# HGRN2 layer of a streaming encoder step: low parts of the heads' outputs made head by head, kept in DRAM and loaded back for the output projection

## The reference

```python
q, f, i, g = split(rms_norm(x) @ w_in[1], 4)          # (544, 2048) @ (2048, 8192)
o = rms_norm(hgrn2(silu(q), (1 - lb) * sigmoid(-f), i, logf, S0)) * silu(g)
x = x + o @ w_out[1]                                  # (544, 2048) @ (2048, 2048)
```

## Time and profile before

| | |
|---|---|
| median of three runs | 2265.87 us (2264.69 to 2266.54) |
| profiled execution, its own time | 2268.73 us |
| its span, first to last instruction | 2267.0 us |
| PE busy | 98% of the span |
| DVE, ACT, POOL busy | 71%, 50%, 3% |
| mean granted clock of PE | 0.994 |
| moved by DMA | 225 MB, a mean of 99 GB/s |

### The profile page before, as it was taken

One profiled execution on the slowest core, in us unless ns is written; L12 is line 12 of the kernel. 1 busy time (PEld: TensorE's weight loads), 2 busy tenths in 40 slices (PEclk: granted clock), 3 DMA queues, 4 the chain that ended last, 5 costly groups with the idle time before them and its releaser, 6 DMA issues.

```text
span 2267.0 us, 43518 instructions
## 1 busy us (share of the span) xinstructions
PE 2213.8 (98%) x17257; PEld 2187.6 (96%) x17257; DVE 1609.6 (71%) x2647; ACT 1138.5 (50%) x1552; POOL 71.5 (3%) x75
## 2 busy tenths in 40 slices
PE   7999999999999999999999999999999999998999
PEld 6999999999999998999999999999999999998999
DVE  7888888888888887522477777777777777776221
ACT  6766566656656666522444444444444444443221
POOL 5000000000000000301000000000000000000000
PEclk9999999999999999999999999999999999999999
DMA  7433333333333336354422222222222222213442
GB/s 257 139 95 95 95 97 108 103 111 95 97 99 98 109 97 192 91 151 115 131 84 70 77 77 77 75 71 78 77 74 72 77 77 77 70 39 100 120 118 81
DMA packets 394470, 224.98 MB, mean 99 GB/s; under 512 B 9523, under 2 KB 378726, under 8 KB 394342
## 3 DMA queue, kind: packets, MB, share of 16 engines
q1 hardware_dynamic: 344342, 189.83, 29.6%
q10 hardware_dynamic: 50032, 33.81, 4.7%
HBM read 195.04 MB, written 28.56 MB: 99 GB/s over the span
## 4 chain that ended last, share of the span: by engine, by line
PE 83%; DVE 7%; ACT 5%; issue 3%; DMA 0%; ACTq 0%; DVEq 0%
PE psum L666 49%; PE psum L873 20%; ACT work L1018 3%; PE psum L789 3%; PE psum L656 2%; DVE work L1583 1%; PE psum L764 1%; PE psum L712 1%; DVE w_lo L1454 1%; PE psum L738 1%; DVE w_chain L1474 1%; PE psum L748 1%; ACT w_hi L1018 1%; PE psum L835 1%; PE psum L814 1%
## 5 line engine op out<-in xcount | busy, mean ns | idle before, releaser
L666 PE MATMUL psum<-act_hi,w_hi 128*128 128x272 f32 x3200 | 678.7, 293 | 9.9 <-DVE act_lo L1540 5.3
L666 PE MATMUL psum<-act_lo,w_hi 128*128 128x272 f32 x3200 | 662.5, 288 | 0.0
L666 PE MATMUL psum<-act_hi,w_lo 128*128 128x272 f32 x3184 | 661.0, 289 | 0.0
L1018 ACT ACTIVATE w_hi<-w_raw 128x1024 fp32r<-128x1024 f32 x350 | 366.2, 1055 | 452.3 <-PE psum L666 256.7
L666 PEld LDWEIGHTS psum<-act_hi,w_hi 128*128 128x128 f32 x3200 | 504.7, 190 | 12.5 <-DVE act_lo L1540 4.3
L666 PEld LDWEIGHTS psum<-act_lo,w_hi 128*128 128x128 f32 x3200 | 505.0, 189 | 0.0
L666 PEld LDWEIGHTS psum<-act_hi,w_lo 128*128 128x128 f32 x3184 | 499.9, 190 | 0.0
L1448 DVE TENSOR_TENSOR w_lo<-w_raw,w_hi 128x1024 fp32r<-128x1024 f32 x199 | 249.1, 1252 | 304.7 <-ACT w_hi L1018 304.5
L1018 ACT ACTIVATE work<-work 128x544 f32<-128x544 f32 (+6 forms) x336 | 235.1, 732 | 285.9 <-DVE work L1698 189.2
L873 PE MATMUL psum<-act_hi,w_hi 128*128 128x272 f32 x960 | 278.7, 290 | 1.8 <-DVE w_lo L1454 1.0
L873 PE MATMUL psum<-act_hi,w_lo 128*128 128x272 f32 x960 | 276.9, 288 | 0.0
(11 more groups left out here) (271 smaller groups left out, 3133.8 us busy)
## 6 DMA issues: line engine op xcount, KB each, us to landing
w_raw<-in_w_in SPq DMA_DIRECT2D x241, 512.0 KB, 4.1
w_raw<-in_w_out SPq DMA_DIRECT2D x64, 512.0 KB, 6.4
out<-work ACTq DMA_DIRECT2D x48, 256.0 KB, 4.4
x_residual<-work ACTq DMA_DIRECT2D x32, 272.0 KB, 3.7
work<-x_residual SPq DMA_DIRECT2D x32, 272.0 KB, 3.0
w_chain<-in_w_in SPq DMA_DIRECT2D x15, 512.0 KB, 4.5
full<-x_residual SPq DMA_DIRECT2D x8, 544.0 KB, 7.2
o_spill<-work ACTq DMA_DIRECT2D x15, 272.0 KB, 2.1
```

The source lines that it names most:

```text
L666: mm = pe.matmul(acc[par][:, j, :], at, a[:, k, j * HT:(j + 1) * HT], start=(k == 0 and n == 0), stop=(k == KT - 1 and n == 2))
L1018: return nc.scalar.activation(out, in_, f, **kw)
```

## The change

ACT and DVE now make the low part of head h's output in the loop, when the head is done: `put_o_lo` on ACT makes the high part into a tile of its own (`o_part_hi`), `o_lo_part` on DVE subtracts it from the output into `o_part_lo`, and ACT issues a store of that to a new DRAM tensor `o_lo_spill`. SP loads the low parts of heads 0 to 14 back into `act_lo`, in four loads of up to 4 heads each, between the third and the fourth half of w_out, once the input projections are done and the store of the heads in question has landed. PE waits for these loads (`o_back`) and for `act_hi` in place of `act_lo_ready`. DVE's 15 low parts beside the last head are gone; ACT still makes the 15 high parts there, and k tile 15 is made as before. The DMA scratch area is set to 8192 bytes.

```diff
--- before.py
+++ after.py
@@ -96,9 +96,6 @@
              {-1: [], 0: [], 1: range(0, 4), 2: [4, 5], 3: [6, 7, 8], 4: [9, 10], 5: [11, 12], 6: [13, 14]}]
 
 
-LAST_REST = {0: range(0, 4), 1: range(4, 8), 2: [8, 9], 3: [10, 11], 4: [12], 5: [13, 14]}
-
-
 class Chain:
 
 
@@ -128,6 +125,7 @@
                  hgrn_norm_w, hgrn_lb, y_prompt, y_sample, k_prompt, v_prompt, s_prompt, k_sample, v_sample,
                  s_sample):
     x_residual = nc.dram_tensor("x_residual", (KT, P, T), F32, kind="Internal").ap()
+    o_lo_spill = nc.dram_tensor("o_lo_spill", (H, P, T), F32, kind="Internal").ap()
     o_spill = nc.dram_tensor("o_spill", (H, P, T), F32, kind="Internal").ap()
 
     with ExitStack() as ctx:
@@ -154,6 +152,8 @@
 
         Y = sb("Y", [P, 4, T])
         rstd_x = sb("rstd_x", [P, T])
+        o_part_hi = sb("o_part_hi", [P, T], F32R)
+        o_part_lo = sb("o_part_lo", [P, T], F32R)
 
         ident = sb("ident", [P, P])
         ident_b = sb("ident_b", [P, P], BF16)
@@ -328,6 +328,7 @@
 
         o_ready = sem("o_ready"); o_stored = sem("o_stored"); o_back = [sem(f"o_back{i}") for i in range(4)]
         run_on_ready = sem("run_on_ready")
+        o_part_hi_ready = sem("o_part_hi_ready"); o_part_lo_ready = sem("o_part_lo_ready")
 
         x_back = [sem(f"x_back{i}") for i in range(4)]; row_scaled = sem("row_scaled")
         diff_made = sem("diff_made"); diff_hi_ready = sem("diff_hi_ready"); diff_lo_ready = sem("diff_lo_ready")
@@ -546,6 +547,14 @@
                                 load_o(u)
                         else:
                             half(i * 4 + (out0 + u), u, src)
+                        if l == 1 and first and u == 2:
+                            sp_eng.wait_ge(half_done, OUT_BASE[1])
+                            for m in range(4):
+                                heads = slice(4 * m, min(4 * m + 4, H - 1))
+                                sp_eng.wait_ge(o_stored, 16 * (H - 1 + heads.stop))
+                                sp_eng.dma_start(act_lo[:, heads, :].bitcast(F32),
+                                                 o_lo_spill[heads].rearrange("k p t -> p k t")
+                                                 ).then_inc(o_back[m], 16)
                     if l == 0 and first:
                         load_o(2)
                         load_o(3)
@@ -658,7 +667,13 @@
             def part(slot, par, ks, wait_act=None, first_lo=False):
 
                 for k in ks:
-                    if wait_act is not None:
+                    if wait_act == 3 * KT:
+                        pe.wait_ge(act_hi_ready, wait_act + k + 1)
+                        if k < KT - 1:
+                            pe.wait_ge(o_back[k // 4], 32)
+                        else:
+                            pe.wait_ge(act_lo_ready, wait_act + 1)
+                    elif wait_act is not None:
                         pe.wait_ge(act_lo_ready, wait_act + k + 1)
                     for n, (w, a) in enumerate(((w_hi, act_hi), (w_hi, act_lo), (w_lo, act_hi))):
                         for j in range(2):
@@ -1246,6 +1261,15 @@
                 act.wait_ge(r_cum, h + 1)
                 func(eb, cum, ACT.Exp).then_inc(r_eb, 1)
 
+            def put_o_lo(h):
+
+                act.wait_ge(o_ready, h + (H + 1))
+                func(o_part_hi[:], full[:, bass.ds(h, 1), :].rearrange("p a t -> p (a t)"), ACT.Copy
+                     ).then_inc(o_part_hi_ready, 1)
+                act.wait_ge(o_part_lo_ready, h + 1)
+                act.dma_start(o_lo_spill[bass.ds(h, 1)].rearrange("a p t -> (a p) t"), o_part_lo[:].bitcast(F32)
+                              ).then_inc(o_stored, 16)
+
             def rec_norm(h):
 
                 act.wait_ge(r_ssq, h + 1)
@@ -1357,6 +1381,7 @@
                             rec_next(h + 1, u)
                             if u == 7:
                                 rec_decays(h + 1)
+                                put_o_lo(h)
                         ch.leave(H - 1)
 
                 g0 = OUT_BASE[l]
@@ -1768,6 +1793,13 @@
                 group(h, 0, 1)
                 dve.wait_ge(r_kde, h + 1)
                 dve.tensor_tensor(kd, kd, kk, ALU.mult).then_inc(r_kd, 1)
+
+            def o_lo_part(h):
+
+                dve.wait_ge(o_part_hi_ready, h + 1)
+                dve.wait_ge(o_stored, h * 16 + 16 * (H - 1))
+                dve.tensor_tensor(o_part_lo[:], full[:, bass.ds(h, 1), :].rearrange("p a t -> p (a t)"),
+                                  o_part_hi[:].bitcast(F32), ALU.subtract).then_inc(o_part_lo_ready, 1)
 
             def rec_dve(h, u):
                 if u == 0:
@@ -1976,6 +2008,7 @@
                             if u == 7:
                                 rec_gate(h)
                                 rec_distances(h + 1)
+                                o_lo_part(h)
                         ch.leave(H - 1)
                     evacuate(l, H - 1, 3)
                 g0 = OUT_BASE[l]
@@ -1991,8 +2024,6 @@
                         rec_dve(H - 1, u)
                     if l == 0 and u == -1:
                         act_split(KT, range(DVE_SPLITS))
-                    elif l == 1 and u in LAST_REST:
-                        act_split(3 * KT, LAST_REST[u])
                     if u == 1:
                         lo(g0 + 3, 3)
                     if u == 4 - l:
@@ -2001,7 +2032,8 @@
                         lo(g0 + 5, 1)
                 if l == 1:
                     rec_gate(H - 1)
-                dve.wait_ge(act_lo_ready, (2 * l + 2) * KT - 1)
+                if l == 0:
+                    dve.wait_ge(act_lo_ready, (2 * l + 2) * KT - 1)
                 act_split((2 * l + 1) * KT, [KT - 1])
 
                 def out_pair(l, i, first=False, last=False):
@@ -2041,7 +2073,7 @@
     import concourse.bacc as _bacc
     from concourse.bass_utils import run_bass_kernel_spmd as _run
 
-    nc = _bacc.Bacc("TRN2", target_bir_lowering=False, num_devices=1)
+    nc = _bacc.Bacc("TRN2", target_bir_lowering=False, num_devices=1, dynamic_dma_scratch_size=8192)
     arrays, args = {}, []
     for name in _INS:
         a = _np.ascontiguousarray(inputs[name])
```

## The result

The changed kernel takes 2272.3 us in the median of 9 runs (2269.46 to 2274.43), the kernel before 2266.69 us in 9 runs beside it. The ratio is 1.0024 with a 95% interval of 1.0015 to 1.0034: 5.4 us slower, between 3.4 and 7.7 us. The forecast was 2269.5 us, 3.6 us slower, which was counted as "no change that can be told". The measured time lies inside the stated range (2264.0 to 2273.5 us), but above the forecast's own (2267.5 to 2270.4 us). The profiled execution took 2272.3 us with a span of 2270.6 us.

The account below looks back on a forecast made before the run. PE's waits in the tail after the loop were taken as the bound. The late fourth half costs 4.4 us, less 0 to 1.6 us of low clock: 2265.87 + 3.6 = 2269.5 us, range 2264.0 to 2273.5 us.

Parts of the forecast that it names:

- What bounds the kernel: PE's waits in the tail, the 53 us after the loop: 11.7 us, nowhere else; DVE's low parts some 5.2 us of the chain.
- What it adds in the loop: Per looped head: ACT's Copy, wait and store issue, DVE's subtraction; ACT 2.4 us late, absorbed by idle time, cost nothing.
- What it adds in the tail, on ACT: Ahead of ACT's first tail work: Copy, wait for DVE's subtraction and store issue move everything on ACT by 2.4 us.
- What it moves on SP: Fourth w_out half queues behind the reloads and head 14's store in the tail, landing at about 2048.7.
- L: Time the fourth w_out half lands in the tail: forecast 2048.7, upper bound 2050.4, lower bound 2046.4.
- The sum: Tail, up to the third level scores: 4.4 us later, less 0 to 1.6 us of low clock; middle 3.6 us.
- behind that nothing changes: After the third level scores: no further change, as last low parts lie in DVE's waits and later chains start at PE.
- Of the 5.2 us taken away nothing is left: Tail: 2.4 us of the relief goes to ACT's delay, the rest was never alone on the path.
- Faster: Rival, tail: DVE's low parts are the bound; 5.2 us plus 1.5 us of low clock return, 2259.2 us; chance 0.10.
- Slower: Rival, ACT's high part in the tail: fourth half lands still later, cost 4.6 to 6.2 us, 2271.3 us; chance 0.31.
- In between: Rival, tail: store shares engines with the loads, half lands at 2046.4, cost 0.6 to 2.2 us, 2267.3 us; chance 0.15.
- Slower in the loop: Rival, loop: ACT's wait for DVE reaches PE in each head, 1 us each, 2281 us; chance 0.04.

Follow-up runs that it names:

- e10: The kernel before with the tail's 15 low parts left out and nothing in their place (result wrong): ratio 0.9985 to the kernel before.
- e2: e1 with the wait for the low part and the store's issue moved from ACT to SP: ratio 0.9984 to the kernel before.
- e1: The changed kernel with SP issuing the fourth w_out half ahead of the four reloads of low parts: ratio 1.0007 to the kernel before.
- e3: The kernel before plus only the loop's new steps; low parts stored, never loaded, and made again in the tail: ratio 1.0012 to the kernel before.
- e9: e2 with the fifth half's split later, its low part behind the third-level placing, and ACT's high parts 4 to 7 behind the kd copies: ratio 0.9961.
- e5: The changed kernel with head 14's low part made by DVE in the tail, so SP's last reload needs no wait for its store: ratio 1.0003.

## Why the prediction was right or wrong

With these runs the tail's 4.70 us can be taken apart by differences: the relief alone is -4.88 (e10); the loop's steps and the reloads, with the store on SP and the half early, +1.49 (e2 less e10); ACT's wait for DVE and its issue of the store +3.48 (e1 less e2); the half behind the reloads +4.61 (the change less e1). The sum is +4.70 by construction. By the ratios the same parts are -3.4, -0.2, +5.2 and +3.9 us, each with some 3 us of doubt. So the signs of the relief, of ACT's delay and of the late half stand, their sizes within 1 or 2 us; the +1.49 isn't shown.

**What bounds the kernel: right.** Waits appeared and went in the tail alone. In the whole loop of the HGRN2 layer PE shows no wait in the kernel before, after, in e1, e2, e3 or e9.

**What it adds in the loop, costed at nothing: right.** The cover was what the step named: ACT's 3.59 us ahead of the third half's high part fell to 1.04 (2.55 us, where 2.4 were taken), DVE's 3.15 to 0.60. There is 0.6 to 1 us of cover left. Moving the store to SP brought no wait of PE in the loop either. The smaller DMA scratch, taken at nothing too, wasn't tried alone.

**What it adds in the tail, on ACT, 2.4 us: right.** The copies of v start 6.43 us after the turns, before 3.80: 2.6 us.

**What it moves on SP: right, to half a microsecond.** L was put at 2048.7, 17.8 us after the turns of v; the half landed 18.2 us after them (2041.96 + 6.06). The store of head 14 took 5.91 us, where 5.8 were taken and 2.1 was the other end. The doubt between "one behind the other" and "shared engines" was put at 2.3 us (2048.7 less 2046.4; worked out again, 4.98 MB at 370 GB/s from 2032.4 on end at 2045.9, so it was 2.8), and in e5, which takes SP's wait for the store away (and 0.27 MB of reloads), the half came 2.3 us sooner. ACT's wait is 4.17 us (some 4 forecast), PE's new wait 5.91 (some 5), the sums over the own scores come 5.0 us later (4.4). e1 confirms the step by undoing it: 4.61 of 4.70 us.

**The sum, "the third level scores run 4.4 us later, less 0 to 1.6 us": this is the step that failed.** They run 5.98 us later against the turns of v. The term that I subtracted was the low clock, "which now would fall earlier, on L814". It fell earlier, as forecast, but it didn't end there: the granted clock is 0.50 from 2048 to 2058, all the way through L829, L833 and the k tiles behind, where the earlier trace rows has it for the 2 us after the wait only. From L833 to the third level scores it takes 15.08 us, before 14.13. The term had the wrong sign, +1.0 us instead of -0.8. The other 0.6 us are the landing (0.4) and the way from there to the own sums (0.2). What the clock costs shows in the k tiles between: at 0.50, 20 matmuls run in 4.00 us (2054 to 2058); at 0.95, 15 run in 2.00 us. Behind the third level scores 1.28 us come back, as the clock is low for a shorter time there than in the profiled execution of before. The step "behind that nothing changes" didn't have that either, and e3, e5 and e10 show the same 1.3 to 1.5 us there, so it more likely belongs to that one execution of before than to the change. That makes the 4.70 us of the tail, against 3.6 forecast: a miss of 2.4 us at the third level scores, and it is luck that half of it was made up behind them.

**"Of the 5.2 us taken away nothing is left … the rest was never alone on the path": right for the waits, without the clock.** In e10 only 1.9 of the 5.2 us come back as a wait, ahead of the own sums. The wait ahead of the third level scores is 2.66 us with and without the low parts, since there the fifth half's high part waits for PE, as the prediction says. What it left out is the low clock behind the wait that shrinks, 1.5 us more up to the third level scores. The rival "Faster" had the low parts as the bound, with 5.2 us and 1.5 us of clock; e10 shows its clock and 1.9 of its 5.2 us. e2 nearly meets its two conditions, with the half there in time and ACT 0.5 us late instead of 2.6, and gains 3.4 us in the tail and 3.6 by the ratio, about half of the 6.7 that the rival named. My sum didn't depend on this, since it followed the chain of the change itself, from the store to the third level scores, and not the difference of a relief and a loss.

**The rivals.** "Slower" came true in its number: 5.4 us lie within its 4.6 to 6.2 us, past the 4.5 us that bound my forecast. It was to decide "once L is past 2048.8 to 2050.4, depending on the clock". Against the turns of v the half landed at 2030.91 + 18.2 = 2049.1, 0.4 us later than forecast, and the clock gave nothing back, so the lower bound of that condition holds. By the prediction's own formula that is 2049.1 - 2044.25 = 4.9 us. What moved the result from the forecast to this rival is the clock, 1.8 us of it, more than the landing. "In between" fell with the store's 5.91 us. "Slower in the loop" fell by the empty list of waits.

**What stays open.** Why the low clock behind one and the same wait of 2.66 us cost 1.3 to 1.5 us more in the kernel before than in four others isn't shown, and with one profile of each kernel it can't be told how often that happens. The 3.48 us between e1 and e2 are 2.1 us of ACT's delay and 1.4 us that may be this. That the reloads would cost less as smaller pieces wasn't tried.

## What to carry to other kernels

When work is replaced by a round trip through memory, look at the reload's place in its queue first: what is issued behind a wait for the newest store inherits that wait and the bulk ahead of it, and a half that had 39 us of room came 4 us late until one line put it ahead. Here the reloads also slowed the store that the last of them waits for: 272 KB took 2.1 us without reloads beside them (e3) and 5.91 with. Take the step away altogether, without its replacement, in one run (as e10 does): it tells what the relief is worth and whether a loss is a missing relief or a new cost. And a wait of PE is to be priced with the matmuls behind it at half clock: here 1.9 us of wait removed brought 3.4 us up to the third level scores. But matmuls at half clock cost nothing where PE ends up waiting anyway, as e1 against e2 shows: a busy time that grows isn't yet a cost.

## What the runs showed that I had not expected

After the 5.9 us wait of the changed kernel PE's granted clock was 0.50 for 10 us (2048 to 2058), although PE was busy in 4.00 of the last 4 of them; the wait had ended at 2050.09. In the kernel before it was back at 0.96 from 2052 on, after a wait of 2.71 us that ended at 2048.88. A store of 272 KB takes 2.1 us in the loop, and in e3 in the tail too, but about 6 us beside the reloads, whether in ACT's queue (5.91) or in SP's (6.53). And DVE's instructions with two inputs in SBUF take up to 3 times as long beside POOL's subtractions (3.40 us for 1.14), and the kernel in which POOL helps takes 1.0018 times as long as the one before.
